# A streaming encoder step on one core: half-wise group norm, fused layer norms, and a deeper ring for one of two gathers

## The reference

```
proj = x @ w_in                                  # q,k,v, indexer, z, xBC, dt, gates: 9060 columns
attn = top-k sparse attention(q, k, v, indexer)  # causal by chunks of 64 keys
y    = SSD scan(silu(conv(xBC)), dt) + d_skip * xs
y    = y * silu(z)
yg   = y.reshape(.., 4 groups, 512)
y    = yg * rsqrt(mean(yg^2) + eps) * norm_w     # group norm of the scan
mix  = sig(g_a) * (attn @ w_attn_br) + sig(g_m) * (y @ w_ssm_br)
h    = LN1(alpha * x + mix @ w_out)
s1,s2 = (h @ wq) against two tables of 128 keys  # 8 heads; top 16 of each, top 16 of the 256 pairs
act  = gelu(h . u[expert])                       # 128 experts for each token
out  = LN2(alpha * h + sum(gate * act * v[expert]))
```

## Time and profile before

| | us |
|---|---|
| three runs | 1749.95, 1745.9, 1750.43 |
| median | 1749.95 |
| the profiled execution | 1746.99 |
| its span | 1745.2 |

### The profile page before, as it was taken

The page is one execution under the profiler, slowest core; times in us unless marked ns, Lnnn a source line. Parts: engine busy times, 40 slices in busy tenths (PEclk is TensorE's granted clock), DMA queues, the critical chain, the costliest instruction groups (busy, mean ns, idle before and its releaser), DMA issues.

```text
span 1745.2 us, 20306 instructions
## 1 busy us (share of the span) xinstructions
PE 1402.6 (80%) x7309; PEld 654.4 (37%) x7309; DVE 1039.9 (60%) x2599; ACT 496.5 (28%) x1239; POOL 795.7 (46%) x818
## 2 busy tenths in 40 slices
PE   8999998889899778879889989788788945566554
PEld 7644554347533323333357433234333311111110
DVE  3423364257686663843677792874925799854555
ACT  1031553012122344631222113454422222221111
POOL 0010073025331675643445323675734467777773
PEclk9999998999999888889999999789998986866887
DMA  8985475769999999999999999999999999999996
GB/s 290 365 269 171 157 229 170 263 241 409 409 409 409 404 409 409 378 378 383 398 409 408 409 409 385 367 409 389 384 378 392 330 378 410 409 410 409 409 409 277
DMA packets 202792, 625.20 MB, mean 358 GB/s; under 512 B 16632, under 2 KB 43960, under 8 KB 202508
## 3 DMA queue, kind: packets, MB, share of 16 engines
q0 software_dynamic: 112784, 410.17, 60.1%
q1 hardware_dynamic: 89908, 213.74, 33.4%
HBM read 611.62 MB, written 12.23 MB: 357 GB/s over the span
## 4 chain that ended last, share of the span: by engine, by line
PE 46%; DVE 18%; DMA 17%; POOL 9%; issue 5%; ACT 5%; SPq 0%; DVEq 0%; POOLq 0%; ACTq 0%
PE banks L705 18%; POOL BIG L609 9%; PE banks L678 9%; DVE BIG L1501 7%; DMA wbuf<-in_w_in_dram 6%; DMA BIG<-in_peer_v_dram,BIG 6%; DMA BIG<-in_peer_u_dram,BIG 5%; PE banks L646 5%; PE banks L771 4%; ACT BIG L1124 3%; PE banks L745 2%; PE banks L1018 1%; PE banks L975 1%; ACT L1124 1%; DVE BIG L1849 1%
## 5 line engine op out<-in xcount | busy, mean ns | idle before, releaser
L646 PE MATMUL banks<-BIG 64*64 64x512 f32 x3072 | 455.3, 709 | 214.0 <-DMA BIG<-in_peer_v_dram,BIG 118.2
L609 POOL DMA_INDIRECT BIG<-in_peer_v_dram,BIG x384 | 368.2, 959 | 437.8 <-PE banks L646 346.0
L1501 DVE CUSTOM_DVE_ANT_0 BIG<-BIG,banks 128x1024 f32<-128x1024 f32 x384 | 459.1, 1217 | 167.4 <-DMA BIG<-in_peer_u_dram,BIG 164.1
L609 POOL DMA_INDIRECT BIG<-in_peer_u_dram,BIG x384 | 367.1, 956 | 269.8 <-DVEq L1892 114.1
L705 PE MATMUL banks<-wbuf,BIG 128*128 128x512 f32 x832 | 385.8, 618 | 16.4 <-DMA wbuf<-in_w_in_dram 8.5
L646 PEld LDWEIGHTS banks<-BIG 64*64 64x64 f32 x3072 | 107.6, 147 | 515.0 <-issue 287.7
L1124 ACT ACTIVATE BIG<-banks 128x512 f32<-128x512 f32 (+5 forms) x255 | 131.4, 544 | 439.8 <-PE banks L678 133.1
L705 PEld LDWEIGHTS banks<-wbuf,BIG 128*128 128x128 f32 x832 | 159.4, 197 | 237.0 <-issue 204.7
L1124 ACT ACTIVATE BIG<-cst,small 128x64 f32<-128x64 f32 (+1 forms) x480 | 142.1, 349 | 347.1 <-DVE small L1490 345.0
L678 PE MATMUL banks<-wbuf,BIG 128*128 128x512 f32 x320 | 151.3, 629 | 2.5 <-ACT BIG L1124 2.5
L1124 ACT ACTIVATE small<-small 128x2 f32<-128x2 f32 (+1 forms) x204 | 41.3, 204 | 383.5 <-DVE small L1501 380.3
(11 more groups left out here) (169 smaller groups left out, 1004.7 us busy)
## 6 DMA issues: line engine op xcount, KB each, us to landing
wbuf<-in_w_in_dram SPq DMA_DIRECT2D x108, 1024.0 KB, 11.2
wbuf<-in_w_ssm_br_dram SPq DMA_DIRECT2D x24, 1024.0 KB, 5.9
wbuf<-in_peer_wq_dram SPq DMA_DIRECT2D x24, 1024.0 KB, 7.8
wbuf<-in_w_attn_br_dram SPq DMA_DIRECT2D x12, 1024.0 KB, 8.7
wbuf<-in_w_out_dram SPq DMA_DIRECT2D x12, 1024.0 KB, 7.3
out_s_ssm_dram<-BIG SPq DMA_DIRECT2D x16, 512.0 KB, 3.8
BIG<-in_peer_u_dram,BIG POOLq DMA_INDIRECT x384, 9.3
BIG<-in_peer_v_dram,BIG POOLq DMA_INDIRECT x384, 9.2
```

Source lines behind the costliest of these rows:

```text
L609: pool.indirect_dma_start(slot, None, table, bass.IndirectOffsetOnAxis(ap=eidx[:, col:col + 1], axis=0)).then_inc(done, 16)
L646: last = mm(acc[i][64 * half:64 * half + 64, :], dg[rows, :], vslot[k][rows, 512 * half:512 * half + 512], start=(b % BLOCKS == 0 and j == 0),
L1501: nc.vector.tensor_tensor_reduce(uslot[s], uslot[s], normed[:, :], 1.0, 0.0, ALU.mult, ALU.add, dots[k % 2][:, j:j + 1]).then_inc(dot_done, 1)
```

## The change

Six edits.

1. The group norm goes in halves. The root and the division of groups 0 and 1 (`mean_roots(0)`, `normalise_y(0)`) are done while the last group of the scan is still under way; PE transposes them, runs the first 32 matmuls of `ym`, and only then transposes groups 2 and 3. The ticks of `yT` and `ym` move into the middle of those matmuls, and that of `mixedT` ahead of its transposes. In the last pass the 16 transposes of the state stand between the halves of `ym`.
2. SP loads the second half of `w_ssm_br` ahead of the layer norm's constants and of `x`.
3. `layer_norm` has two fused instructions for each half of 512 columns, with a semaphore count for each half; the `bn_stats` of a half are taken as soon as it is there. The transposes and the last stores go by halves. The second layer norm has a third set of small buffers.
4. The ring of `u` has four blocks, that of `v` still three.
5. `v` is gathered two blocks behind `u`, not one.
6. The tables `adm` and `nadm` (1536 columns of constants) give way to `chunks` (128 columns), and the masking of the index scores is done on 128 columns.

```diff
-RING = 3
-SLOTS = RING * WB
+RING, VRING, VLAG = 4, 3, 2
+SLOTS, VSLOTS = RING * WB, VRING * WB
...
-    parts["adm"] = adm
-    parts["nadm"] = (1 - adm) * NEG
+    parts["chunks"] = t[None, :] // CHUNK <= t[:, None] // CHUNK
...
 SP:
                 for b in range(2):
                     load_wide(a["w_ssm_br"][0][D * b:D * (b + 1)], 0, (vb_filled, at["ym"][0] + 2) if b else None)
-                    if b:
+                    if not b:
+                        if q.first:
+                            sample_states(q)
                         continue
-                    if q.first:
-                        sample_states(q)
                     if q.t == 1:
-                        sp.wait_ge(sb_drained, SR + before[n, "yT"][1])
+                        sp.wait_ge(sb_drained, SR + before[n, "yT"][1] + 6)
...
-                    sp.wait_ge(rms_root, n + 1)
+                    sp.wait_ge(rms_root, 2 * (n + 1))
...
 POOL:
-                c = b - 1
+                c = b - VLAG
                 if 0 <= c < TOTAL:
                     for j in range(WB):
-                        if c >= RING:
-                            pool.wait_ge(v_used, WB * (c - RING) + j + 1)
-                        k = c % RING * WB + j
+                        if c >= VRING:
+                            pool.wait_ge(v_used, WB * (c - VRING) + j + 1)
+                        k = c % VRING * WB + j
                         gather(table_v, vslot[k], WB * c + j, v_in[k])
...
 PE:
+                def turn_y(half):
+                    for quarter in (2 * half, 2 * half + 1):
+                        pe.wait_ge(yn_ready, G * q.n + quarter + 1)
+                        rows_to_T(y, quarter)
+                    s_written()
+
+                phase("yT")
+                turn_y(0)
+                dsts = wide_tile(yTv[:, 0:KC, :], vf, vbank, lambda: step("yT"), end=False)
+                step("ym")
                 if t == 1:
-                    v_written()
                     for quarter in range(4):
                         rows_to_T(stateT, quarter)
-
-                phase("yT")
-                step("yT")
-                for quarter in range(4):
-                    pe.wait_ge(yn_ready, G * q.n + quarter + 1)
-                    rows_to_T(y, quarter)
-                s_written()
-                phase("ym")
-                dsts = wide_tile(yTv[:, 0:KC, :], vf, vbank, None, end=False)
-                step("ym")
-                wide_tile(yTv[:, KC:2 * KC, :], vf, vbank, None, dsts=dsts)
-                step("ym")
-                phase("mixedT")
+                turn_y(1)
+                wide_tile(yTv[:, KC:2 * KC, :], vf, vbank, lambda: step("ym"), dsts=dsts)
+                step("mixedT")
...
-                pe.wait_ge(h_ready, q.n + 1)
                 for half in range(2):
+                    pe.wait_ge(h_ready, 2 * q.n + half + 1)
                     rows_to_T(H[q.n], half)
...
 ACT, in the scan's loop over g and after it:
+                    if g == 2:
+                        mean_roots(0)
                     step("y")
+                keep_yT(0)
+                square(G - 1)
+                mean_roots(1)
+                step("yT")
...
+                keep_yT(1)
...
 DVE:
-                own(tsc(v, v, mv[:, 0:1], rs[:, 1:2], ALU.subtract, ALU.mult))
-                own.settle()
-                own(tt(v, v, g, ALU.mult))
-                own.settle()
-                tt(o, v, b, ALU.add).then_inc(final, 1)
+                for half in range(2):
+                    c = slice(half * 512, (half + 1) * 512)
+                    own(stt(v[:, c], v[:, c], mv[:, 0:1], g[:, c], ALU.subtract, ALU.mult))
+                    own.settle()
+                    stt(o[:, c], v[:, c], rs[:, 1:2], b[:, c], ALU.mult, ALU.add).then_inc(final, 1)
...
                     if g + 1 < G:
                         decays(g + 1)
+                    else:
+                        normalise_y(0)
                     own.step.upto(dve)
                     src = bank()
                     own(tt(yg, yg, src[:, :], ALU.add), vd)
```

More of the change, by code:

```diff
@@ L231, in build @@
         uslot = [take(D) for _ in range(SLOTS)]
-        vslot = [take(D) for _ in range(SLOTS)]
+        vslot = [take(D) for _ in range(VSLOTS)]
         H = [take(D) for _ in range(TILES)]
@@ L338, in build @@
         ms, rstd = tiny(8), tiny(8)
-        norms = [(tiny(12), tiny(2), tiny(2)) for _ in range(2)]
+        norms = [(tiny(12), tiny(2), tiny(2)) for _ in range(3)]
         dots, gl, w8 = ([tiny(WB) for _ in range(2)] for _ in range(3))
@@ L1313, in square, with mean_roots, keep_yT @@
                     f(squares[:, g * 512:(g + 1) * 512], y[:, g * 512:(g + 1) * 512], ACT.Square, accum_out=ms[:, g:g + 1]).then_inc(ms_ready, 1)
+                def mean_roots(half):
+                    act.wait_ge(ms_ready, G * q.n + 2 * half + 2)
+                    f(rstd[:, 2 * half:2 * half + 2], ms[:, 2 * half:2 * half + 2], ACT.Sqrt, scale=1.0 / 512,
+                      bias=eps).then_inc(rms_root, 1)
+                def keep_yT(half):
+                    for quarter in (2 * half, 2 * half + 1):
+                        src = bank()
+                        for i in range(4):
+                            c = 4 * quarter + i
+                            last = f(yTv[:, c, :], src[:, i * P:(i + 1) * P], scale=normT[:, c:c + 1])
+                        sd.give(last)
                 if q.first:
@@ L1356, in mixer @@
                         sd.give(f(pso[:, quarter * 512:(quarter + 1) * 512], src[:, :]))
-                square(G - 1)
-                act.wait_ge(ms_ready, G * (q.n + 1))
-                f(rstd[:, 0:G], ms[:, 0:G], ACT.Sqrt, scale=1.0 / 512, bias=eps).then_inc(rms_root, 1)
-                for quarter in range(4):
-                    src = bank()
-                    for i in range(4):
-                        c = 4 * quarter + i
-                        last = f(yTv[:, c, :], src[:, i * P:(i + 1) * P], scale=normT[:, c:c + 1])
-                    sd.give(last)
-                step("yT")
+                keep_yT(1)
                 for _ in range(2):
@@ L1448, in bc, with half_stats @@
                 return ap.to_broadcast([P] + list(shape))
+            def half_stats(v, which, half):
+                own.settle()
+                own(nc.vector.bn_stats(norms[which][0][:, 6 * half:6 * half + 6], v[:, half * 512:(half + 1) * 512]))
             def layer_norm(v, o, n, which, g, b, ready, done, final):
                 bns, mv, rs = norms[which]
-                for half in range(2):
-                    own(nc.vector.bn_stats(bns[:, 6 * half:6 * half + 6], v[:, half * 512:(half + 1) * 512]))
                 own.settle()
```

68 lines of the change are left out of this document (34 added, 34 removed).

## The result

Over 20 runs of the changed kernel, beside 20 of the kernel before, the median is 1737.9 us against 1747.8: ratio 0.9951, 95% interval 0.9934 to 0.9967. In twelve later runs it was 0.9950 (0.9927 to 0.9973). By the ratio the change is worth 8.6 us; I had forecast 20.7. The direction was right, and the median lies in the wide range (1714 to 1742), but outside the 1722 to 1735 that I had given 0.52; the size was wrong.

What follows compares the result with a forecast made beforehand. No engine alone was taken as the bound; gathers, lost DMA time and PE's path before the first gather set the end. Gains of 10.0 + 3.8 + 6.0 + 0 + 0.9 = 20.7 us gave 1726.3, stated as 1728; range 1714 to 1742.

Steps and rivals of the forecast that it cites:

- First pass, norm, 5.5 us.: Scan to `out`: `ym` starts 6.9 us earlier, a second stop costs 3.2, better clock returns 2.0; taken as 5.5.
- First pass, layer norm, 2.8 + 0.8.: Last `out` work to `wq`: 2.8 us from fused, halved instructions, 0.8 from a better PE clock.
- Constants, 0.9.: First pass: 0.72 MB less of constants to load shortens PE's wait for the weights behind it by 0.9 us.
- Followed through to the start of `out`, PE is 4.4 us ahead in the second and 4.0 in the third.: Scan to `out`, later passes: `ym` starts 6 and 8 us earlier; after moved ticks and second stop, 4.4 and 4.0 remain.
- Layer norm in the later passes, 3.6 each.: After `out` in the second and third pass: 2.8 us from the layer norm and 0.8 from its clock.
- Third pass, 6.0 us.: PE's path up to the indices at 1390 is 6.0 us shorter, all of it won from 16.0 us of lost DMA time.
- The added table load, 1.6 us off each later pass.: `mean_roots(0)` adds a table load of 1.28 us and a root of 0.3 on ACT's path.
- Second pass, 3.8 us.: 698 to 879 us: of 11.1 us lost DMA time, 6.4 is won by PE's path and 2.6 held back; 3.8 gained.
- Ring 0, held v 2.6.: From 1390 us the fourth `u` block wins 2.6, cancelling 2.6 of held `v`; each index wait moves 2.56 us of work.
- End, 0.9.: After the last gather: fused instructions save 0.5 us and a store of half the size about 0.4.
- The DMA engines taking it back: Rival: in later passes PE arrives sooner and waits; only first pass and end count, 10.9 us, 1739; chance 0.22.
- Weights crowded out: Rival: one more `u` block queued delays weight tiles PE waits for; 25 us slower, 1775; chance 0.05.

Runs made afterwards that it cites:

- e5_ln: The kernel before with only the layer norms changed: ratio 0.9995 to the kernel before.
- e3_noring: The changed kernel without its buffers (three blocks of `u`, `v` one block behind): ratio 0.9974 to the kernel before.
- e12_after: The changed kernel itself again, unaltered, for a second profile and more runs: ratio 0.9950 to the kernel before.
- e2_ringmask: The kernel before with only four blocks of `u`, `v` two blocks behind and the smaller mask: ratio 1.0000 to the kernel before.
- e4_tick: The changed kernel with DVE's second `ym` tick moved ahead of the mixing: ratio 0.9902 to the kernel before.
- e8_tickv: e4_tick with the waiting blocks of `v` issued ahead of each index wait: ratio 0.9883 to the kernel before.
- e11_lag1: e4_tick with four blocks of `u` but `v` gathered one block behind: ratio 0.9922 to the kernel before.
- e14_best: The same kernel as e9_best, run again: ratio 0.9887 to the kernel before.
- e6_lnord: e4_tick with DVE's dots and ACT's gelu of the last `out` tick moved behind the layer norm: ratio 0.9876 to the kernel before.
- e7_ticknr: e4_tick with the buffers of before (three blocks of `u`, `v` one behind): ratio 0.9941 to the kernel before.
- e9_best: The changed kernel with the repairs of e4_tick, e6_lnord and e8_tickv together: ratio 0.9870 to the kernel before.
- e13_state: e9_best with the third pass's transposes of the state, their copies and store moved behind the last scores: ratio 0.9859, repeated 0.9853, to the kernel before.
- e16_fill3: e13_state with three and two matmuls on zeros in PE's waits ahead of `ym`'s halves, later passes only: ratio 0.9848 to the kernel before.

## Why the prediction was wrong, by its steps

- *First pass, norm, 5.5 us.* The mechanism was right and at full clock worth 6.5. The profiles of the changed kernel show 3.5 and 5.1, the rest lost to half clock. I had counted the clock as a gain on the ground of one pause that PE had got through at 1.00.
- *First pass, layer norm, 2.8 + 0.8.* 2.0 at `wq`, 1.0 at the first gather (e5_ln). Scan to first gather as a whole: 7.6 us less where there is no half clock up to `out` (96.7 to 89.0, e3_noring); the 9.1 forecast for norm and layer norm fell short here alone by 1.5.
- *Constants, 0.9.* PE's wait for the weights behind that load fell from 0.92 to 0.48 us, and to 0.17 and 0.26 in e12_after and e2_ringmask: 0.4 to 0.75.
- *"Followed through to the start of `out`, PE is 4.4 us ahead in the second and 4.0 in the third."* This is the step that failed. It left a stop of 4.3 us for the mixing, where it stayed at 7.2 to 7.5 (once 5.9); before, it was 7.0 and 7.5. I had moved PE's ticks and not asked which tick on DVE each one needs. In the second pass that is 3.2 of the 4.9 us that are missing at `out`; the other 1.7 is half clock in the first half of `ym`, 17.8 us where it takes 16.1 at full clock. The changed kernel's `out` starts 0.5 and 0.2 us later behind the second scan than before, in two profiles, and 0.7 later and 0.6 sooner behind the third. e4_tick moves one instruction of 0.15 us and two dot products ahead of the mixing and gets both stops down to 3.6 us, and the whole from 8.6 to 17 us under before.
- *Layer norm in the later passes, 3.6 each.* 0.6 and 0.2: they come from the same kind of oversight, and are the second step that failed. The root waits for the gelu and the table load. The shadow that I took as free was the path. The load took 1.28 us and the root followed after 0.02, as in the earlier trace rows; the longer price of the Trainium skill ("ScalarE: Activation LUTs", "What ACT_TABLE_LOAD costs") did not show here either.
- *Third pass, 6.0 us.* From index wait to index wait it took 1.2 us less than before in one profile and 4.9 more in the other (509.6 and 515.7 against 510.8). The two steps above are one cause, the clock is another: with the tick repaired, scan to `out` was 50.2 us where PE had 2.0 to 2.4 us of half clock on the way (e8_tickv, e11_lag1, e14_best), and 55.2 or 55.3 where it had 10.2 (e4_tick, e6_lnord, e7_ticknr, e9_best). Before, it was 54.7 with 10.4, and 53.0 with 5.6 in e2_ringmask, which has the order of before. So the repair is worth 2.8 to 4.5 us there in a quick execution and nothing in one with 10 us of half clock. Before, part of the half clock fell on the waits and transposes ahead of `ym`, whose first half lost 2.0 us by it; in e9_best it fell on the matmuls of both halves, which lost 4.6. The transposes of the state, 2.75 us, I had within the stop of 5.5 us; e13_state shows that they could leave it.
- *The added table load, 1.6 us off each later pass.* The page counts 99 loads where it had 97, and from the first gather to the end of the second scan it took 376.4 and 373.3 us where it was 378.2: no cost shows there. For the third pass (386.4 and 393.2 against 385.1) it stays open.
- *Second pass, 3.8 us.* It gave 2.3 and 5.7 in the two profiles (first gather to index wait 500.5, now 498.2 and 494.8), but not by the step named; what gave it, these runs don't isolate.
- *Ring 0, held v 2.6.* Alone 0 (e2_ringmask). But with the rest the ring is likely worth 4 to 7 us, and the held v costs about 3.3 in all, not 2.6 twice.
- *End, 0.9.* Last matmul to the end of the span fell from 11.7 to 10.6 us: right.
- *The rivals.* The DMA engines taking it back comes nearest in time (1739), by luck: time taken off PE's path in the later passes reaches the end (e4_tick and the two other pairs with its edit), and the path had hardly become shorter. Weights crowded out: in the second pass PE came to the matmuls of `dt` 3 us later behind the first gather (85.1 against 82.1 us), and by the end of attention the difference was 0.8 us. In the third pass it came 5.3 us later (88.0 against 82.7), and the scan ended 1.3 us later behind the index wait in one profile and 8.1 in the other. The delay at `dt` is real and goes with the deeper ring (e3_noring: 82.2 and 79.8); paid back in the second pass, it may cost something in the third. No run separates that, and over all the ring did not lose.
- *The last sum.* 1726.3 and the 3.0 us to the median's scale are 1729.3; I wrote 1728. Nothing hangs on it.

The best versions measured are e13_state (medians 1722.5 and 1723.2 us) and e16_fill3 (1718.0, in the same session as the second), not distinguished by their ratios: nearly three times the gain of the change.

## What to carry to other kernels

Where small tasks of several engines are woven into a main program, following one engine's program through a change is not enough: for each task that now stands ahead of the main work, find the task on the next engine that feeds it, and what that one stands behind. An engine idle for 28 us in front of a queue head that waits for something else is the sign. And a step that lies beside a table load or another engine's wait earns little when it is made faster (here 0.2 to 0.6 us of 3.6); ask which of the two ends last before counting it.

## What the runs showed of the hardware

PE's granted clock moved one stage by as much as most edits did: between the third scan and `out` one kernel had 10.2 us of half clock in one execution (e9_best) and 2.0 in another (e14_best), and the way took 55.2 and 50.2 us. With PE kept busy in its waits the clock was 1.00 from the second scan to `out` (e16_fill3), and the half clock up to 1390 us was 133 us against 136 without the fillers. A rise of the clock in one stretch is not a gain until the end of the program shows it. An indirect gather of 0.52 MB holds POOL for 0.94 us, and the next follows after 0.30 (e8_tickv).
